# Building the residual by DRAM-to-DRAM copies and accumulating DMAs instead of storing it from SBUF

## The reference, cut to what matters

```python
xs = x_sample + grid_position_embedding(x_sample.shape[1], D_MODEL)[None]
# in trunk_layer, for both groups of tokens:
h = rms_norm(x, norm_mix_g) * (1 + sc_a) + sh_a
proj = h @ w_in                       # pooling heads, z, conv channels, dt
...                                   # pooling heads and two SSD scans
x = x + g_a * (jnp.concatenate([y_pool, y_ssd], axis=-1) @ w_out)
h = rms_norm(x, norm_ffn_g) * (1 + sc_m) + sh_m
x = x + g_m * expert_choice_ffn(h, ...)
```

## Time and profile before

| | us |
|---|---|
| median of 3 runs | 2225.2 (2224.36 to 2226.51) |
| the profiled execution: its own time | 2223.47 |
| its span, first to last instruction | 2221.6 |
| PE busy | 2140.3 (96%) |
| DVE busy | 1367.0 (62%) |
| ACT busy | 1003.7 (45%) |
| POOL busy | 268.2 (12%) |

### The profile page before, as it was taken

One profiled execution on the slowest core, in us unless ns is written; L12 is line 12 of the kernel. 1 busy time (PEld: TensorE's weight loads), 2 busy tenths in 40 slices (PEclk: granted clock), 3 DMA queues, 4 the chain that ended last, 5 costly groups with the idle time before them and its releaser, 6 DMA issues.

```text
span 2221.6 us, 39700 instructions
## 1 busy us (share of the span) xinstructions
PE 2140.3 (96%) x15666; PEld 1994.6 (90%) x15666; DVE 1367.0 (62%) x2050; ACT 1003.7 (45%) x1760; POOL 268.2 (12%) x383
## 2 busy tenths in 40 slices
PE   5999999998999999799999999999999999999995
PEld 4878888896888888699999999999999999999995
DVE  3758444346888886865655665665556466555564
ACT  4743221125565554444444454454444445444653
POOL 1300000013122221200000000000000000000113
PEclk9999999999999999999999999999999999999998
DMA  9733444367344443356656566565656666566885
GB/s 306 234 103 119 138 146 146 101 214 230 113 140 132 147 157 108 105 174 199 206 164 202 194 179 191 187 217 156 203 191 187 189 188 208 170 191 196 265 312 172
DMA packets 320974, 398.69 MB, mean 179 GB/s; under 512 B 11726, under 2 KB 273758, under 8 KB 319070
## 3 DMA queue, kind: packets, MB, share of 16 engines
q1 hardware_dynamic: 290894, 290.36, 41.0%
q0 software_dynamic: 24960, 97.53, 14.4%
q10 hardware_dynamic: 5024, 9.50, 1.2%
HBM read 320.74 MB, written 77.14 MB: 179 GB/s over the span
## 4 chain that ended last, share of the span: by engine, by line
PE 53%; ACT 2%; DVE 1%; issue 1%; ACTq 0%; DVEq 0%
PE experts_ps_r L2887 50%; PE experts_ps_x L2865 1%; PE experts_ps_o L2875 1%; ACT experts_whi L2968 1%; PE experts_ps_i L2800 1%; ACT experts_junk L3002 0%; DVE experts_wlo L3130 0%; DVE kept_raw L3236 0%; DVE experts_hid L3300 0%; DVE experts_onehot L3141 0%; PE experts_ps_o L2178 0%; DVE experts_xg L3245 0%; DVE experts_xg L3236 0%; DVE experts_kept_c L3227 0%; ACT experts_xhi L3049 0%
## 5 line engine op out<-in xcount | busy, mean ns | idle before, releaser
L3130 DVE TENSOR_TENSOR experts_wlo<-kept_raw,experts_whi 128x2048 fp32r<-128x2048 f32 x192 | 439.8, 2291 | 388.1 <-ACT experts_whi L2968 388.0
L2887 PE MATMUL experts_ps_r<-experts_xhi,experts_whi 128*128 128x272 f32 x2048 | 602.0, 294 | 3.4 <-DVE experts_wlo L3130 2.6
L2887 PE MATMUL experts_ps_r<-experts_xhi,experts_wlo 128*128 128x272 f32 x2048 | 593.2, 290 | 0.0
L2887 PE MATMUL experts_ps_r<-experts_xlo,experts_whi 128*128 128x272 f32 x2048 | 589.3, 288 | 0.0
L2887 PEld LDWEIGHTS experts_ps_r<-experts_xhi,experts_whi 128*128 128x128 f32 x2048 | 385.5, 188 | 4.5 <-issue 2.6
L2887 PEld LDWEIGHTS experts_ps_r<-experts_xlo,experts_whi 128*128 128x128 f32 x2048 | 386.3, 189 | 0.0
L2887 PEld LDWEIGHTS experts_ps_r<-experts_xhi,experts_wlo 128*128 128x128 f32 x2048 | 385.1, 188 | 0.0
L2968 ACT ACTIVATE experts_whi<-kept_raw 128x2048 fp32r<-128x2048 f32 x192 | 366.1, 1907 | 0.0
L2887 PE MATMUL experts_ps_r<-experts_hhi,experts_whi 128*128 128x272 f32 x1024 | 302.0, 295 | 3.5 <-DVE experts_hlo L3303 3.5
L2887 PE MATMUL experts_ps_r<-experts_hhi,experts_wlo 128*128 128x272 f32 x1024 | 296.8, 290 | 0.0
L2887 PE MATMUL experts_ps_r<-experts_hlo,experts_whi 128*128 128x272 f32 x1024 | 295.4, 288 | 0.0
(11 more groups left out here) (549 smaller groups left out, 3207.2 us busy)
## 6 DMA issues: line engine op xcount, KB each, us to landing
kept_raw<-in_w_gate SPq DMA_DIRECT2D x64, 1024.0 KB, 5.3
kept_raw<-in_w_up SPq DMA_DIRECT2D x64, 1024.0 KB, 5.4
kept_raw<-in_w_down SPq DMA_DIRECT2D x64, 1024.0 KB, 5.3
shared_whalf<-in_w_ada SPq DMA_DIRECT2D x16, 1024.0 KB, 5.1
ssd_mz<-mixed SPq DMA_DIRECT2D x17, 768.0 KB, 8.8
mixed<-front_acc POOLq DMA_DIRECT2D x12, 1024.0 KB, 4.3
ssd_xs<-resid SPq DMA_DIRECT2D x17, 512.0 KB, 4.0
early_wa<-in_w_ada ACTq DMA_DIRECT2D x4, 2048.0 KB, 21.2
```

The lines of the kernel that those rows point to most:

```text
L2887: mm = pe.matmul(dst, w[:, c % RING, kk, cols], r[:, kk, :], start=(kk == 0 and q == 0), stop=(kk == KD - 1 and q == 2))
L3130: dve.tensor_tensor(wlo[:, c % RING, :, :], raw[:, c % RAW, :, :], whi[:, c % RING, :, :].bitcast(F32), ALU.subtract).then_inc(wlo_done, 1)
```

## The change

POOL's additions in `early_xin` stay, but nothing is stored from there. After its last addition POOL issues four 2 MB copies of x_sample and one 512 KB copy of x_prompt, memory to memory, into `resid`. After each of the eight conv stores it issues, for two tiles of 128 tokens, two accumulating DMAs each (256 KB: the row half with a broadcast source, the column half with a repeated one), 32 in all; the first of them waits for all five copies. SP's load of x loses its wait on the store; conv 0 loses its wait on all stores; the end of the stage waits for the 32 DMAs in place of the stores.

```diff
         def load_x(i):
...
-                if i >= 3:
-                    sp.wait_ge(xs_stored[b], 16 * (i // 2))
                 if i >= 2:
                     sp.wait_ge(xn_done, i - 1)
...
-            def store_x(i):
+            def add_rows(i):
                 b = i % 2
                 pool.wait_ge(x_loaded[b], 16 * (i // 2) + 16)
                 pool.wait_ge(pos_loaded[b], 32 * ((i + 1) // 2))
                 pool.tensor_tensor(xin[:, b, 0:512], xin[:, b, 0:512], prow[:, b, :], ALU.add).then_inc(row_added, 1)
-                pool.wait_ge(row_added, i)
-                pool.wait_ge(pos_added, i)
-                pool.dma_start(io["resid"][P * i:P * i + P, :], xin[:, i % 2, :]).then_inc(xs_stored[i % 2], 16)
 
             for i in range(1, NT):
-                store_x(i)
-                if i == 2:
-                    pool.dma_start(io["resid"][0:P, :], x_ctx).then_inc(xs_stored[0], 16)
+                add_rows(i)
+            LAT_PART = LAT // 4
+            for n in range(4):
+                rows = slice(LAT_PART * n, LAT_PART * n + LAT_PART)
+                pool.dma_start(io["resid"][CTX + LAT_PART * n:CTX + LAT_PART * n + LAT_PART, :], x_lat[rows, :]).then_inc(resid_copied, 16)
+            pool.dma_start(io["resid"][0:CTX, :], x_ctx).then_inc(resid_copied, 16)
+
+            def place_rows(n):
+
+                rows = io["resid"][CTX + P * n:CTX + P * n + P, :].rearrange("(r c) d -> r c d", c=GRID_W)
+                per_row = io["pos_row"][2 * n:2 * n + 2, :].unsqueeze(1).broadcast_to([2, GRID_W, 512])
+                per_col = io["pos_col"].unsqueeze(0).broadcast_to([2, GRID_W, 512])
+                if n == 0:
+                    pool.wait_ge(resid_copied, 80)
+                pool.dma_start(rows[:, :, 0:512], per_row, accum_op=ALU.add).then_inc(resid_placed, 16)
+                pool.dma_start(rows[:, :, 512:D], per_col, accum_op=ALU.add).then_inc(resid_placed, 16)
...
             for t in range(8):
                 store("conv", t, t % 2, acc, acc_stored[t % 2], (silu_done, t + 1))
+                for n in range(2 * t, 2 * t + 2):
+                    place_rows(n)
...
-                pool.wait_ge(xs_stored[b], 16 * ((NT + 1 - b) // 2))
                 pool.wait_ge(acc_stored[b], 32 * 6)
+            pool.wait_ge(resid_placed, 32 * (NT - 1))
...
                     dve.wait_ge(xt_done, turned_event(NT - 1))
-                    for n in range(2):
-                        dve.wait_ge(xs_stored[n], 16 * ((NT + 1 - n) // 2))
```

More of the change, by code:

```diff
@@ L352, in front @@
         x_loaded, pos_loaded, pcol_loaded = k.sems("x_loaded", 2), k.sems("pos_loaded", 2), k.sem("pcol_loaded")
-        xs_stored = k.dma_sems("xs_stored", 2)
+        resid_copied, resid_placed = k.dma_sem("resid_copied"), k.dma_sem("resid_placed")
         row_added = k.sem("row_added")
```

## The result

The changed kernel takes 2251.99 us (median of 4 runs, 2248.25 to 2253.21). The kernel before took 2224.78 on the same chip (4 runs, 2222.88 to 2226.51). The ratio is 1.0117, with a 95% interval of 1.0105 to 1.0128. I had forecast 2222.7 and a range up to 2231, so the change is slower by 27 us where I expected nothing measurable. The profiled execution took 2248.25 us, its span is 2246.4.

A forecast was written before the change was run, and what follows sets the result against it. PE was taken to bound the kernel, so only its waits in `front` (6.7 us) could change. 2223.5 - 3.0 (x stage) + 0.5 (collisions) = 2221.0, plus 1.7 for the median of runs gives 2222.7; range 2217.5 to 2231.

The forecast's parts named there:

- The x stage: Chain of loads and additions before the columns: 1.9 (store wait gone), 0.6 (POOL's waits gone), 0.5 (less traffic), 3.0 us gained.
- The wait of 1.69 us at chunk 3: PE's stand for the last tile's low part; tile 11's earlier load was to save 1.9 us of chain, bounds 0 and 3.6.
- the 0.5 of the traffic: 8.4 MB of stores leave the x stage, so loads land sooner: 0.5 us of chain, bounds 0 and 1.5.
- the twelve and the ten: Loads of x in the earlier trace: twelve last released by the scaling, ten by a store, 20.2 us in total.
- The copies: Five memory-to-memory copies, 8.9 MB, after the last addition: 24 us at 366 GB/s, ending at 147 us, covered, value 0.
- The accumulating DMAs: Four behind each conv store: 6.2 us of all 16 engines a group, value 0; 0.5 us allowed for collisions of both new kinds.
- the window: Load of shared_whalf in a column, issued at 220.66 and used at 231.38: 10.7 us for a landing of 5.1.
- The 3.3 us of overlap: At most this much of a group of four falls on the load of shared_whalf, which then lands after 8.4 us.
- Rival A: Accumulating DMAs hold part of the engines longer, shared_whalf lands late in six columns; 2237, extremes 2226 and 2263; chance 0.14.
- A's middle of 2237: Middle case of the late shared_whalf: landing at 13.1 us, 2.4 x 6 = 14.4 us lost, added to 2222.7.
- The waits: Conv 0's wait on all stores was long met; the stage's end waits for DMAs issued by 340 us: cost nothing.

The follow-up runs named there:

- column_first: The changed kernel, complete, with the same 32 accumulating DMAs written with the 64 grid columns as slowest dimension and the two grid rows inside; 2219.01 us, ratio 0.9964.
- copies_only: The changed kernel without the 32 accumulating DMAs, so positions are missing from the residual; 2219.91 us, ratio 0.9974.
- plain_two_dims: The changed kernel with the same 32 DMAs written without addition into scratch tensor x2, so positions are missing from the residual; 2220.68 us, ratio 0.9978.

## Why the prediction was wrong

**The x stage: right, a size off.** Forecast 3.0 us, measured 4.1. The wait of 1.69 us at chunk 3 went, as worked out: the start of chunk 3 gains 1.9 us more than that of chunk 1 (114.93 to 110.76 and 72.77 to 70.50). On the way from the first product to chunk 1 it is 0.7 us, where a wait of 0.7 us at 52 us is down to 0.2; the wait at chunk 1 itself is 2.59 us as before, and the clock of 70 to 80 us is 0.83 in both. The largest surprise lies before that: the first product starts 1.6 us earlier (48.63 to 47.04), for which I had at most the 0.5 of the traffic. As to that term, the two kernels that keep it gain 1.7 us less than the mean of those without, as far as single traces tell.

One reading was wrong without harm: the earlier trace rows counts stands, not loads. Thirteen loads go out from 40 to 126 us. SP stood for the scaling before twelve of them and once more for the store of x before ten, so the twelve and the ten are not different loads.

**The copies: right.** I had 24 us at 366 GB/s, done at 147. They began earlier, at 116.3 us, since POOL no longer waits for DVE, and took 29.9 us, up to 146.2; they moved 479 GB/s at first and less later:

```profile
120.00:124.00 4.00, 4.00 (x23) 3.32 (x22) 2.88 (x7) 3.14 (x9) 0.00 (x0) 1.00 1.33 479
...
124.00:140.00 16.00, 16.00 (x78) 11.70 (x77) 3.82 (x6) 4.45 (x8) 0.00 (x0) 1.00 1.03 336
140.00:150.00 10.00, 10.00 (x44) 7.85 (x42) 0.00 (x0) 1.07 (x2) 0.00 (x0) 1.00 0.41 139
```

The column load went out at 144.62 and nothing waited for it. I had looked for the loads near the copies and not for the stores; ACT's store of z was the near one.

**The accumulating DMAs: the step that failed.** "So a group of four (1 MB) costs 6.2 us of all 16 engines" and, of the half, "It lands after 8.4 us, inside the window." It was taken from DMAs of another shape, with two assumptions: that all 16 engines carry them, and that they cost what those cost. The second was near for the pieces: column_first, which does use all engines, needs 6.9 us of them for the pieces of a group. The first failed: in the trace half the engines carry a group, and the small packets come on top, 12.0 + 3.8 = 15.8 us of eight engines in place of 6.2 of sixteen. The 3.3 us of overlap that I worked out became an overlap with the whole load: landing 14.3 us in place of 8.4, 3.6 beyond the window at most; PE's longest wait was 4.1. The total, 19.3 us over six waits, is 3.2 a column.

**The second omission: the clock.** Rival A counted the late landings alone: 2.4 x 6 = 14.4 us. Four of the six stands of PE were followed by products at 1.2 GHz, and the loss is 9.1 us together, nearly half as much again as the waits. The earlier trace rows had shown the same behind a stand of 2.59 us, and I used it for the gain and not for the loss. With it, 14.4 would have been 14.4 x 28.4 / 19.3 = 21 us.

The sum with measured terms: 2223.5 - 4.1 + 28.4 = 2247.8 us, against 2248.25 for the profiled execution.

**The chances.** Rival A is what happened: six columns, a landing beyond 10.7 us, half the engines. I gave it 0.14, with the argument that 30 accumulating DMAs of the trace landed in 6.3 us. That was no evidence on this shape, and I had written so myself: no row showed a DMA with such a source. The range should have reached through A's middle of 2237 to its far side. The Trainium skill ("DMA: Bandwidth & Descriptors", section "Why a DMA increments its semaphore by 16 and not by 1") states that a DMA runs on the largest number of engines up to 16 that divides the slowest dimension of both sides, which is two for each of these DMAs. The trace agrees for a group of four, with shares of 0.50 to 0.56 at 224 and 235 us, and column_first with 0.98. I had named that rule ahead of the rivals and gave the rival that follows from it 0.14.

**The waits: right, as far as shown.** With the old waits gone from conv 0 and a wait for the copies at the end, the stretch of copies_only is as long as that of before. The wait for the 32 DMAs at the end stands in the changed kernel and in column_first, whose stretch (145.21 to 520.22 us) is 375.0 us against 374.9.

## What to carry to other kernels

Look at the outermost dimension of both sides of a DMA before you price it by bytes: with 2 there, 256 KB took 13.5 to 15.3 us, with 64 there 7.9 to 9.1, at the same bytes, pieces and place. Price a DMA by a row with the same shape, and where there is none, let the range hold the bad case. When a load may miss its window, add to the expected stands of TensorE what its clock may lose behind them: here nearly half of their sum, lost behind four of six.

## What the runs showed of the hardware

- An accumulating DMA took about twice as long as the plain one with equal shape and bytes: 13.5 against 6.9 us, 15.3 against 8.2.
- A slowest dimension of 2 adds packets under 512 B: 28672 more for the changed kernel than for column_first, which is 7 for each of the 4096 pieces of 2 KB. They have 8 bytes and take 8 ns each. The plain DMAs of the same shape (plain_two_dims) have half as many, 14336. What they are isn't shown.
- GpSimd stood at the issue of a DMA behind earlier ones with 2 outermost, up to 15.5 us behind seven of 256 KB; with 64 outermost, 16 went out without a stop.
- A stand of TensorE of 2.9 or 3.0 us was followed by a granted clock of 0.50, one of 3.5 us was not.
- A store of 256 KB from ACT's queue was held for 10.5 and 15.6 us while 8.9 MB were copied from memory to memory on another queue.
